# Latent attention with its queries and keys made token by token, latent norms as token factors, and the in-projection's tiles in another order

## The chip, the cores and the metric

One core of a Trainium2 chip runs the whole program; nothing is shared with other cores. The metric is the device time of one execution in microseconds, a median over runs. The engines are named as in the profile: PE (matrix products; PEld is its weight load), DVE and ACT (elementwise work), POOL (here it only splits weights), SP (a queue that issues DMA).

## The reference

A residual stream x of 512 tokens and 1024 channels passes through two layers of a first block (attention with an indexer, two recurrences, SwiGLU networks) and two layers of a second. The change lies in the first layer of the second block, in its latent attention (`mla_qkv` and the short convolution beside it):

```python
p_lat, p_ctx = h_lat @ w_in, h_ctx @ w_in          # 512 and 256 tokens; 384 + 256 + 32 latent columns, 3 x 512 for the convolution
q  = (rmsnorm(cq,  q_norm_g)  @ w_uq ).reshape(B, T, 8, 96)
kv = (rmsnorm(ckv, kv_norm_g) @ w_ukv).reshape(B, T, 8, 64 + 64)
k  = concat([k_nope, broadcast(k_pe)])             # 64 columns per head, 32 that all heads share
q, k = rmsnorm(q, q_gain), rmsnorm(k, k_gain)      # over the 96 columns of a head
# latent tokens only: axial rope on the last 32 columns of q and k
# attention of 512 queries over 512 + 256 keys
# short_conv: z = c_gate * u; y = 3 taps of z along tokens; b_gate * y
```

All is float32. A norm of a latent is a factor per token and a gain per column, so the factor can be applied before the following product or after it.

## The kernel before, in words

Activations lie with channels on the partitions: a buffer h has 8 chunks of 128 channels by 512 tokens. Every product is made of three (`products`, lines 1810 to 1815): operands are split in a rounded high part and the remainder, and high x high, high x low, low x high are added in PSUM. Weights come as one stream of tiles of 128 x 1024 (512 KB). SP loads tile t into slot t % 4 of `w_raw` once `w_used` says that the tile four places back was consumed (line 445); ACT rounds it to `w_hi` (`round_tile`, L480), at a place in ACT's program written out by hand; POOL subtracts and gives `w_lo` (L458). PE takes a tile with 24 products of 512 columns (`linear_tile`).

Latent attention is the functions `mla` of ACT (from line 897), DVE (1660) and PE (2411). The order on each engine is written out by hand, and the engines meet in semaphores.

**In-projection**, 18 tiles, in order 0 to 17. After the norm of x, `first_tiles` makes tiles 0 and 1. PE then adds the squares of the 8 context chunks with a product with ones (L2419). From that sum ACT takes a root (L912), DVE a reciprocal (L1668) and scales and shifts the context (L1670, L1673), ACT rounds it (L914), DVE subtracts (L1676). Tiles 2, and then 3 to 5, which also have 24 products of 256 columns for the context (`linear_ctx`), follow; ACT evicts each bank (L918, L921). Tiles 0 to 2 are the query latent, 3 and 4 the key and value latent, 5 the shared rope columns. ACT squares both latents (L925, L926), PE adds the squares per token (L2445), ACT and DVE make root and reciprocal (L940, L941, L1682), PE spreads the factors over the partitions (L2458), DVE scales the latents (L1687), ACT rounds (L945, L947), DVE subtracts (L1691). Tiles 6 to 17 are the convolution, three to a group of 128 channels; ACT evicts the first (L935), DVE multiplies it with the second (L1700), makes the taps (L1702, L1704) and multiplies with the third (L1706). Since DVE's work on the latents stands ahead of the first convolution in its program, and PE reuses the banks, tile 10 waits for L1700.

**Queries and keys.** For each of 8 query heads (512 tokens, 9 products) and 8 key heads (768 tokens, 12 products) the weight is the stationary side, so a head comes out with its 96 columns on the partitions. Then per head: ACT evicts (L964, L967) and squares (L975), PE adds the squares per token (L2470), ACT takes the root (L982), DVE the reciprocal (L1724), PE spreads the factor over 96 partitions (L2480), DVE scales (L1728), PE makes the rotated columns (L2490), DVE applies rope with three operations (L1717 to L1719). PE's steps of head i - 1, i - 2 and i - 3 stand behind the products of head i. The key half alone waits on the copy L1709. Then the values: six blocks of 128 tokens as the stationary side, 6 products each (L2532 to L2534), evicted by ACT (L995).

**Attention**, 32 pairs of a token block and a head: scores (L2546, L2547), maximum (L1750, L1751), exponential (L1005), six turns (L2553), product with the values (L2561).

Of the kernel before, what the change touches and what calls it, by code (L numbers as in the profile page):

```python
# [19 lines left out]
P = 128  # L20
T = 512
D = 1024
KD = D // P
# [83 lines left out]
def build_program(nc, io, out):  # L107
# [3 lines left out]
    with ExitStack() as ctx:  # L111
# [238 lines left out]
        ctx_x = flat2[:, 0:KD * CTX].rearrange("p (k t) -> p k t", k=KD)  # L350
        cq = mem2[:, 4:7, :]
        ckv = flat2[:, 7 * T:7 * T + 2 * TK].rearrange("p (c t) -> p c t", c=2)
# [8 lines left out]
        consts2 = core_mem[:, 12:15, :].rearrange("p u t -> p (u t)")[:, 0:N_CONSTS_2]  # L361
# [7 lines left out]
        def qk_width(i):  # L369

            return T if i < 8 else TK


        def qk_tok(i):

            return head_tok[:, KB * (i % 2):KB * (i % 2) + qk_width(i) // P]
# [14 lines left out]
        def ada_cols(layer, part, which=0):  # L391
# [24 lines left out]
            "lat_sq", "lat_sum", "lat_std", "lat_f", "lat_hi", "lat_ready", "c_out", "u_taken", "conv_taken",  # L416
            "qk_ready", "qk_out", "qk_sq", "qk_sum", "qk_std", "qk_inv", "qk_spread", "qk_done", "lat_inv", "lat_spread", "kpe_ready", "rot2_ready", "rot2_done", "vtok_ready", "vtok_out",
# [5 lines left out]
        def _(sp):  # L423
# [18 lines left out]
            with sp.Fori(1, stream_tiles // RING) as i:  # L442
# [19 lines left out]
        def _(act):  # L462
# [434 lines left out]
            def mla(order, updates):  # L897
                base = BASE["mla_in"]

                def load_ctx():  # L900

                    act.wait_ge(S["x_ready"], KD * updates)
                    act.dma_start(ctx_x, io["ctx_t"].rearrange("(k p) t -> p k t", p=P)).then_inc(S["ctx_loaded"], 16)

# [3 lines left out]
                for m in range(6):  # L908
                    if m == 2:

                        act.wait_ge(S["ctx_sum"], 1)
                        nc.scalar.activation(mem2[:, CTX_STD, 0:CTX], ps[:, 6, 0:CTX], ACT.Sqrt, scale=1.0 / D, bias=eps(EPS_NORM)).then_inc(S["ctx_std"], 1)  # L912
                        act.wait_ge(S["ctx_f"], 1)
                        nc.scalar.activation(hc_hi[:, :, :], ctx_x, ACT.Copy).then_inc(S["ctx_hi"], 1)  # L914
                    act.wait_ge(S["w_used"], base + m + 1)
                    bank = ps[:, m % 2, :]
                    out = cq[:, m, :] if m < 3 else ckv[:, m - 3, 0:T] if m < 5 else kpe[:, 0:T]
                    nc.scalar.activation(out, bank, ACT.Copy).then_inc(S["proj_out"], 1)  # L918
                    if m >= 3:
# [1871 lines left out]
```

## Time and profile before

| | us |
|---|---|
| median of 3 runs | 3841.18 (3839.13 to 3841.76) |
| the profiled execution, its own time | 3836.46 |
| its span, first to last instruction | 3834.7 |
| PE busy | 3595.0 (94%) |
| DVE, ACT, POOL busy | 1614.7, 1240.5, 1237.4 |
| latent attention's in-projection, from tile 2 on | 134.2 |
| its queries, keys and values | 124.2 |
| its attention | 114.1 |
| mean granted clock of PE | 0.952 of full |

The profiled execution is 4.7 us below the median of the runs. Times in rows count from the start of the span. PE's durations overlap, since products are pipelined; the distance of two starts is what one costs. "idle before" is the time an engine stood before an instruction, with what ended it. A granted clock of 1.00 is 2.4 GHz, 0.50 is 1.2 GHz.

### The profile page before, as it was taken

Reading aid. Unit: us, or ns where it says so; the run is one execution under the profiler, and the core shown is the slowest. Engines: PE = TensorE matmul, PEld = TensorE weight load, DVE = VectorE, ACT = ScalarE, POOL = GpSimd, SP = SyncE. Lnnn points to the kernel's source line nnn. Section 1 sums busy time; section 2 is a strip of 40 time slices with the busy share of each in tenths; the row PEclk is TensorE's granted clock in tenths of the full one; section 3 lists DMA queues with packets and bytes.
Section 4 is the critical chain, followed back from the end, with each engine's and each line's share of the span. In section 5 each row is a group of like instructions: output and inputs, shape, how many; then the busy total and the mean of one; then the engine's idle time right before and its main releaser. Section 6 shows DMA issues by size and latency. Waiting matters only on the chain.

```text
span 3834.7 us, 46792 instructions
## 1 busy us (share of the span) xinstructions
PE 3595.0 (94%) x17424; PEld 2954.8 (77%) x17424; DVE 1614.7 (42%) x2716; ACT 1240.5 (32%) x1852; POOL 1237.4 (32%) x516
## 2 busy tenths in 40 slices
PE   7999997689999999999778999988899999989999
PEld 6888775588888888877557888867677888777887
DVE  5440596656331433168575533123555221323220
ACT  3222435234222322243522422232233332323331
POOL 3444330004444444433000444423102444323443
PEclk9999996799999999999779999989899999999999
DMA  4442220003442344222000344222001222112222
GB/s 169 148 144 97 77 83 6 1 1 122 143 145 104 138 143 147 93 77 77 6 1 1 127 148 143 104 72 75 26 6 45 103 94 99 66 61 88 94 98 93
DMA packets 93534, 332.08 MB, mean 87 GB/s; under 512 B 10432, under 2 KB 12128, under 8 KB 93280
## 3 DMA queue, kind: packets, MB, share of 16 engines
q1 hardware_dynamic: 77136, 274.65, 20.5%
q10 hardware_dynamic: 16272, 55.65, 4.2%
q8 instruction: 91, 1.49, 0.2%
q14 instruction: 35, 0.29, 0.0%
HBM read 327.64 MB, written 2.62 MB: 86 GB/s over the span
## 4 chain that ended last, share of the span: by engine, by line
PE 86%; DVE 9%; ACT 2%; issue 2%; DMA 1%; SPq 0%; DVEq 0%; ACTq 0%
PE ps L1813 22%; PE ps L1815 21%; PE ps L1814 21%; PE ps L1834 1%; PE ps L1839 1%; PE ps L1835 1%; DMA w_raw<-in_tiles 1%; PE ps L2561 1%; PE ps L1964 1%; PE ps L2116 1%; PE ps L2546 1%; DVE mem L1254 1%; DVE stat L1253 1%; PE ps L1957 1%; PE ps L2295 1%
## 5 line engine op out<-in xcount | busy, mean ns | idle before, releaser
L458 POOL TENSOR_TENSOR w_lo<-w_raw,w_hi 128x1024 fp32r<-128x1024 f32 x512 | 1237.2, 2418 | 2573.8 <-ACT w_hi L480 2573.5
L1813 PE MATMUL ps<-h_hi,w_hi 128*128 128x512 f32 x2656 | 1044.7, 393 | 8.9 <-DVE mem L1700 7.0
L1815 PE MATMUL ps<-h_hi,w_lo 128*128 128x512 f32 x2656 | 1034.9, 390 | 0.0
L1814 PE MATMUL ps<-h_lo,w_hi 128*128 128x512 f32 x2656 | 1034.5, 389 | 0.0
L480 ACT ACTIVATE w_hi<-w_raw 128x1024 fp32r<-128x1024 f32 x512 | 540.8, 1058 | 990.5 <-DMA w_raw<-in_tiles 985.6
L1813 PEld LDWEIGHTS ps<-h_hi,w_hi 128*128 128x128 f32 x2656 | 499.4, 188 | 127.7 <-issue 14.3
L1814 PEld LDWEIGHTS ps<-h_lo,w_hi 128*128 128x128 f32 x2656 | 499.6, 188 | 105.3 <-issue 3.4
L1815 PEld LDWEIGHTS ps<-h_hi,w_lo 128*128 128x128 f32 x2656 | 499.2, 188 | 104.8
L1159 DVE TENSOR_TENSOR a_lo<-sil,a_hi 128x512 f32 (+1 forms) x132 | 298.6, 2262 | 492.7 <-ACT a_hi L622 492.7
L1813 PE MATMUL ps<-a_hi,w_hi 128*128 (+1 forms) x1056 | 410.8, 389 | 0.0
L1814 PE MATMUL ps<-a_lo,w_hi 128*128 (+1 forms) x1056 | 410.8, 389 | 0.0
L1815 PE MATMUL ps<-a_hi,w_lo 128*128 (+1 forms) x1056 | 410.8, 389 | 0.0
L614 ACT ACTIVATE sil<-ps 128x512 f32<-128x512 f32 x129 | 77.1, 598 | 698.9 <-PE ps L1815 690.2
L1157 DVE TENSOR_TENSOR sil<-sil,ps 128x512 f32<-128x512 f32 x129 | 88.7, 688 | 392.9 <-ACT sil L614 392.9
L1814 PEld LDWEIGHTS ps<-a_lo,w_hi 128*128 128x128 f32 x1056 | 198.2, 188 | 41.5
L1813 PEld LDWEIGHTS ps<-a_hi,w_hi 128*128 128x128 f32 x1056 | 198.2, 188 | 40.9
L1815 PEld LDWEIGHTS ps<-a_hi,w_lo 128*128 128x128 f32 x1056 | 198.2, 188 | 40.9
L1188 DVE SCALAR_TENSOR_TENSOR x<-ps,x 128x512 f32<-128x512 f32 x32 | 22.1, 692 | 310.4 <-PE ps L1815 309.8
L1136 DVE SCALAR_TENSOR_TENSOR ada_raw<-ada_raw,sq 128x1024 f32<-128x1024 f32 x96 | 126.2, 1317 | 9.5 <-DMA ada_raw<-in_ada_tiles 9.5
L1834 PE MATMUL ps<-h_hi,w_hi 128*128 128x512 f32 x208 | 87.9, 423 | 17.3 <-DVE h_lo L1082 8.8
L1188 DVE SCALAR_TENSOR_TENSOR x<-ps,ada,x 128x512 f32<-128x512 f32 x16 | 12.0, 751 | 193.0 <-PE ps L1815 193.0
L1835 PE MATMUL ps<-h_hi,w_lo 128*128 128x512 f32 x208 | 85.9, 413 | 0.0
(448 smaller groups left out, 3913.0 us busy)
## 6 DMA issues: line engine op xcount, KB each, us to landing
w_raw<-in_tiles SPq DMA_DIRECT2D x512, 512.0 KB, 3.2
ada_raw<-in_ada_tiles ACTq DMA_DIRECT2D x96, 512.0 KB, 3.2
x<-in_x_t SPq DMA_DIRECT2D x2, 1024.0 KB, 6.5
sq<-in_cond ACTq DMA_DIRECT2D x4, 512.0 KB, 4.2
out_t<-x SPq DMA_DIRECT2D x1, 2048.0 KB, 7.1
consts<-in_consts SPq DMA_DIRECT2D x1, 1280.0 KB, 12.8
mem<-in_ctx_t ACTq DMA_DIRECT2D x1, 1024.0 KB, 8.7
core_mem<-in_consts ACTq DMA_DIRECT2D x1, 576.0 KB, 3.8
```

Of the source, the lines that this page charges most:

```text
L458: nc.gpsimd.tensor_tensor(w_lo[:, s, :], w_raw[:, s, :], w_hi[:, s, :].bitcast(F32), ALU.subtract).then_inc(S["w_lo_ready"], 1)
L480: nc.scalar.activation(w_hi[:, t % RING, :], w_raw[:, t % RING, :], ACT.Copy).then_inc(S["w_hi_ready"], 1)
L614: nc.scalar.activation(sil[:, j, :], ps[:, 2 * j, :], ACT.Silu).then_inc(S["silu_ready"], 1)
L1136: nc.vector.scalar_tensor_tensor(raw, raw, 1.0, cond_rows(n)[0], ALU.mult, ALU.mult, accum_out=ada[:, 0, column]).then_inc(S["ada_used"], 1)
L1157: nc.vector.tensor_tensor(sil[:, j, :], sil[:, j, :], ps[:, 2 * j + 1, :], ALU.mult).then_inc(S["af_ready"], 1)
L1159: nc.vector.tensor_tensor(a_lo[:, 2 * i + j, :], sil[:, j, :], a_hi[:, 2 * i + j, :].bitcast(F32), ALU.subtract).then_inc(S["a_ready"], 1)
L1253: link(nc.vector.max(top, score(n)))
L1813: nc.tensor.matmul(bank, wh, hi, start=first, stop=False, skip_group_check=True)
L1814: nc.tensor.matmul(bank, wh, lo, start=False, stop=False, skip_group_check=True)
L1815: return nc.tensor.matmul(bank, wl, hi, start=False, stop=last, skip_group_check=True)
L1834: nc.tensor.matmul(ps[:, banks[r], :], w_hi[:, slot, block], h_hi[:, k, :], start=(n == 0), stop=False, skip_group_check=True)
L1835: nc.tensor.matmul(ps[:, banks[r], :], w_lo[:, slot, block], h_hi[:, k, :], start=False, stop=False, skip_group_check=True)
```

## The change

Order and buffers of the in-projection: the tiles come in the order 0, 1, 2, 6, 7, 8, 3, 4, 5, 9 to 17 (the SP queue writes out the loads of that stretch, all others stay in loops). Each latent goes to a bank of its own; ACT writes its high part straight from the bank with the norm's gain as the scale, and its squares beside it; DVE makes the low part from the bank (`low_part`). The token factor isn't applied to the latents. DVE adds the context's squares over chunks, so that PE needs one product, and likewise the latents' squares. The tables for rope and their gains are turned to tokens on the partitions by 14 small turns and 2 products of PE into bank 7, and DVE multiplies them with the gains once; the table load is issued on ACT's queue right behind the context's.

Queries and keys: 20 units. A query unit is 128 tokens by 4 heads (384 columns, 9 products, 8 units), a key unit 128 tokens by 8 heads (512 columns, 6 products, 6 units), a value unit as before. Latents are the stationary side, weights the moving one, read in pieces of 96 or 64 columns across two slots. Per unit: ACT squares the bank, DVE sums over a head's columns, ACT takes the root (with the latent's factor as scale, for keys with the shared columns' sum as bias), DVE inverts it and scales the bank into tokens, and applies rope on 32 columns of each head (queries), or multiplies the ready roped key columns by the factor (keys). PE turns each head back to columns on the partitions, two units late, and ACT evicts the turn with the head's gain. The value eviction carries the latent's factor. Weight tiles are rounded by ACT at the units in `rounds`; two or more slots are freed at once by the units in `UNITS_LAST`.

```diff
-        ctx_x = flat2[:, 0:KD * CTX].rearrange("p (k t) -> p k t", k=KD)
...
+        ctx_x = flat2[:, 16 * T:16 * T + KD * CTX].rearrange("p (k t) -> p k t", k=KD)
...
-        consts2 = core_mem[:, 12:15, :].rearrange("p u t -> p (u t)")[:, 0:N_CONSTS_2]
+        consts2 = flat2[:, 4 * T:4 * T + N_CONSTS_2]
...
+        MLA_ORDER = (0, 1, 2, 6, 7, 8, 3, 4, 5, *range(9, 18))
+        LATENT_BANKS = ((0, None), (1, None), (3, None), (4, 6), (5, 7), (4, 6))
+        Q_UNITS, K_UNITS, V_UNITS = 8, KB, KB
+        QK_UNITS = Q_UNITS + K_UNITS
...
+            return (3, 0, 1, 2)[u % 4]
+        UNITS_LAST = {3: 2, 7: 4, 13: 6, 19: 7}
...
+            for t in range(RING * first_group, RING * (last_group + 1)):
+                source = base + MLA_ORDER[t - base] if t in reordered else t
+                sp.wait_ge(S["w_used"], t + 1 - RING)
+                sp.dma_start(w_raw[:, t % RING, :], io["tiles"][source]).then_inc(w_loaded[t % RING], 16)
...
+                def latent(m):
+                    bank, ctx_bank = LATENT_BANKS[m]
+                    if m < 3:
+                        nc.scalar.activation(cq_hi[:, m, :], ps[:, bank, :], ACT.Copy, scale=param("mla_qn", m))
+                        nc.scalar.activation(mem2[:, CQ_STD + m, :], ps[:, bank, :], ACT.Square).then_inc(S["lat_taken"], 1)
+                    elif m < 5:
+                        for part, source in ((slice(0, T), ps[:, bank, :]), (slice(T, TK), ps[:, ctx_bank, 0:CTX])):
+                            nc.scalar.activation(ckv_hi[:, m - 3, part], source, ACT.Copy, scale=param("mla_kvn", m - 3))
+                            ins = nc.scalar.activation(ckv_sq[:, m - 3, part], source, ACT.Square)
+                        ins.then_inc(S["lat_taken"], 1)
...
+                for p, m in enumerate(MLA_ORDER):
+                    act.wait_ge(S["w_used"], base + p + 1)
+                    if m < 6:
+                        latent(m)
+                    elif m % 3 == 0:
+                        j = (m - 6) // 3
+                        if j >= 2:
+                            act.wait_ge(S["u_taken"], j - 1)
+                        nc.scalar.activation(mem2[:, j % 2, :], ps[:, 0, :], ACT.Copy).then_inc(S["c_out"], 1)
+                    if p == 2:
                         act.wait_ge(S["ctx_sum"], 1)
                         nc.scalar.activation(mem2[:, CTX_STD, 0:CTX], ps[:, 6, 0:CTX], ACT.Sqrt, scale=1.0 / D, bias=eps(EPS_NORM)).then_inc(S["ctx_std"], 1)
+                    if p == 3:
                         act.wait_ge(S["ctx_f"], 1)
                         nc.scalar.activation(hc_hi[:, :, :], ctx_x, ACT.Copy).then_inc(S["ctx_hi"], 1)
...
+                    if p < 16:
+                        round_tile(base + p + 4)
...
+                rounds = {0: (2,), 2: (3,), 6: (4,), 7: (5,), 9: (6,), 10: (7,)}
...
+                    if u >= 2:
+                        act.wait_ge(S["qk_sum"], u - 1)
+                    nc.scalar.activation(unit_squares(u), unit_products(u), ACT.Square).then_inc(S["qk_sq"], 1)
+                    act.wait_ge(S["qk_sum"], u + 1)
+                    n = u % TB if u < Q_UNITS else TB + u - Q_UNITS
+                    bias = eps(EPS_NORM) if u < Q_UNITS else kpe_bias[:, n - TB:n - TB + 1]
+                    nc.scalar.activation(unit_sums(u), unit_sums(u), ACT.Sqrt, scale=lat_factor2[:, n:n + 1], bias=bias).then_inc(S["qk_std"], 1)
+                def turned_out(u):
+                    for x, turn in enumerate(turns(u)):
+                        act.wait_ge(S["qk_turned"], turn + 1)
+                        if u < Q_UNITS:
+                            out = mem2[0:QKD, Q_MLA + 4 * (u // TB):Q_MLA + 4 * (u // TB) + 4, blk(u % TB)]
+                        else:
+                            out = kmla[0:QKD, 4 * x:4 * x + 4, blk(u - Q_UNITS)]
+                        gain = gains[0:QKD, int(u >= Q_UNITS):int(u >= Q_UNITS) + 1]
+                        nc.scalar.activation(out, heads(ps[0:QKD, 4 + turn % 4, :]), ACT.Copy, scale=gain).then_inc(S["qk_out"], 1)
...
+                    if 2 <= u < QK_UNITS + 2:
+                        turned_out(u - 2)
+                    for t in rounds.get(u, ()):
+                        round_tile(base + t)
+                for t in (8, 9, 10):
+                    round_tile(base + t)
...
+                    if m < 3:
+                        ins = V.scalar_tensor_tensor(cq_lo[:, m, :], ps[:, bank, :], param("mla_qn", m), cq_hi[:, m, :].bitcast(F32), ALU.mult, ALU.subtract)
+                    else:
...
+                low_part(0)
+                low_part(1)
+                dve.wait_ge(S["ctx_sq"], 1)
+                link(V.tensor_tensor(ctx_sq[:, 0:4, :], ctx_sq[:, 0:4, :], ctx_sq[:, 4:8, :], ALU.add))
+                link(V.tensor_tensor(ctx_sq[:, 0:2, :], ctx_sq[:, 0:2, :], ctx_sq[:, 2:4, :], ALU.add))
+                V.tensor_tensor(ctx_sq[:, 0, :], ctx_sq[:, 0, :], ctx_sq[:, 1, :], ALU.add).then_inc(S["ctx_added"], 1)
+                low_part(2)
...
+                def rope_tokens(x, cos, sin, temp, n):
+                    link(V.tensor_tensor(temp, x, sin, ALU.mult))
+                    link(V.tensor_tensor(x, x, cos, ALU.mult))
+                    V.tensor_tensor(halves(x, 0), halves(x, 0), halves(temp, 1), ALU.subtract)
+                    return V.tensor_tensor(halves(x, 1), halves(x, 1), halves(temp, 0), ALU.add)
...
+                conv(0)
+                low_part(3)
+                low_part(4)
+                square = lambda c: mem2[:, CQ_STD + c, :]
+                link(V.tensor_tensor(square(0), square(0), square(1), ALU.add))
+                V.tensor_tensor(square(0), square(0), square(2), ALU.add)
+                V.tensor_tensor(ckv_sq[:, 0, :], ckv_sq[:, 0, :], ckv_sq[:, 1, :], ALU.add).then_inc(S["lat_added"], 1)
...
+                for u in range(QK_UNITS):
+                    h, inv, tok, source = unit_heads(u), unit_sums(u), unit_tokens(u), unit_products(u)
+                    n = u % TB if u < Q_UNITS else TB + u - Q_UNITS
+                    factor = lat_factor[:, n:n + 1]
+                    dve.wait_ge(S["qk_sq"], u + 1)
+                    V.reduce_sum(inv, unit_squares(u), AX_X).then_inc(S["qk_sum"], 1)
+                    dve.wait_ge(S["qk_std"], u + 1)
+                    link(V.reciprocal(inv, inv))
+                    if u >= 2:
+                        dve.wait_ge(S["qk_turned"], turns(u - 2)[-1] + 1)
+                    spread = lambda w: inv.unsqueeze(2).to_broadcast([P, h, w])
+                    if u < Q_UNITS:
+                        V.scalar_tensor_tensor(tok, source, factor, spread(QKD), ALU.mult, ALU.mult).then_inc(S["qk_scaled"], 1)
+                        dve.wait_ge(S["qk_scaled"], u + 1)
+                        rope_tokens(tok[:, :, HD:QKD], over(cos_gain[:, n, :], h), over(sin_gain[:, n, :], h), by_head(rope_temp, 4), h).then_inc(S["qk_done"], 1)
+                    else:
+                        V.scalar_tensor_tensor(tok[:, :, 0:HD], source, factor, spread(HD), ALU.mult, ALU.mult).then_inc(S["qk_scaled"], 1)
+                        V.tensor_tensor(tok[:, :, HD:QKD], over(kpe_roped[:, n - TB, :], h), spread(32), ALU.mult).then_inc(S["qk_done"], 1)
...
+                    if p == 3:
+                        pe.wait_ge(S["ctx_added"], 1)
+                        nc.tensor.matmul(ps[:, 6, 0:CTX], const("ones"), ctx_sq[:, 0, :], start=True, stop=True).then_inc(S["ctx_sum"], 1)
+                    if m < 6:
+                        bank, ctx_bank = LATENT_BANKS[m]
+                        if m >= 3:
+                            pe.wait_ge(S["ctx_ready"], 1)
+                            pe.wait_ge(S["w_lo_ready"], t + 1)
+                            if m == 5:
+                                pe.wait_ge(S["lat_lo"], 4)
+                            linear_ctx(ps[:, ctx_bank, 0:CTX], t)
+                        linear_tile(ps[:, bank, :], t)
+                    else:
+                        j, part = (m - 6) // 3, (m - 6) % 3
+                        if j == 0 and part < 2:
+                            pe.wait_ge(S["lat_lo"], part + 1)
+                        if j:
+                            pe.wait_ge(S[("c_out", "u_taken", "conv_taken")[part]], j)
+                        linear_tile(ps[:, part, :], t)
...
+                    if u >= 4:
+                        if u - 4 < QK_UNITS:
+                            pe.wait_ge(S["qk_scaled"], u - 3)
+                        else:
+                            pe.wait_ge(S["vtok_out"], u - 4 - QK_UNITS + 1)
...
+                        half, n = divmod(u, TB)
+                        pe.wait_ge(S["w_lo_ready"], base + 2 * half + 2)
+                        out = bank[:, 0:4 * QKD].rearrange("p (s h d) -> p s h d", s=2, h=2)
+                        weights = lambda w, k: w[:, 2 * half:2 * half + 2, 0:6 * P].rearrange("p s (h k m) -> p s h k m", h=2, k=3)[:, :, :, k, 0:QKD]
+                        chunks, hi, lo = 3, cq_hi, cq_lo
...
+                    for k in range(chunks):
+                        nc.tensor.matmul(out, hi[:, k, blk(n)], weights(w_hi, k), start=(k == 0), stop=False)
+                        nc.tensor.matmul(out, hi[:, k, blk(n)], weights(w_lo, k), start=False, stop=False)
+                        ins = nc.tensor.matmul(out, lo[:, k, blk(n)], weights(w_hi, k), start=False, stop=(k == chunks - 1))
+                    if u in UNITS_LAST:
...
+                def turn(u):
+                    pe.wait_ge(S["qk_done"], u + 1)
+                    for x, slot in enumerate(turns(u)):
+                        if slot >= 4:
+                            pe.wait_ge(S["qk_out"], slot - 3)
+                        for h in range(4):
+                            ins = nc.tensor.transpose(ps[0:QKD, 4 + slot % 4, blk(h)], unit_tokens(u)[:, 4 * x + h, :], const("ident"))
+                        ins.then_inc(S["qk_turned"], 1)
...
+                for u in range(QK_UNITS + V_UNITS):
+                    if u == 1:
+                        pe.wait_ge(S["c_out"], 4)
+                    if u == 2:
+                        pe.wait_ge(S["u_taken"], 4)
+                    if u == 3:
+                        pe.wait_ge(S["conv_taken"], 4)
+                    products_of(u)
+                    if 2 <= u < QK_UNITS + 2:
+                        turn(u - 2)
...
```

## Rows read from the trace of the kernel before

**Rows 1.** The page: the chain that ended last, share of the span by engine

```profile
PE 86%; DVE 9%; ACT 2%; issue 2%; DMA 1%; SPq 0%; DVEq 0%; ACTq 0%
```

**Rows 2.** Stretches: length, busy us (count) per engine, granted clock, DMA share, GB/s

```profile
2531.50:2665.70 134.20, 114.08 (x542) 96.20 (x540) 34.93 (x49) 32.26 (x38) 40.68 (x17) 0.91 0.19 67
...
2665.70:2789.90 124.20, 108.70 (x556) 81.73 (x556) 55.20 (x81) 35.61 (x61) 17.96 (x8) 0.89 0.11 35
...
2789.90:2904.00 114.10, 109.47 (x720) 89.47 (x720) 67.36 (x104) 35.62 (x70) 2.34 (x1) 0.99 0.02 6
...
740.00:760.00 20.00, 13.77 (x122) 13.15 (x121) 16.00 (x56) 4.04 (x9) 0.00 (x0) 0.83 0.00 1
...
1890.00:1970.00 80.00, 49.88 (x213) 35.91 (x211) 44.24 (x125) 32.32 (x51) 0.00 (x0) 0.59 0.02 7
```

**Rows 3.** Timeline, PE, in-projection: start us, us, instruction, [idle before <-releaser]

```profile
2531.45 3.62 PE L2419 MATMUL ps<-mem,consts 128*128 128x256 f32 x16
...
2551.12 0.55 PE L1813 MATMUL ps<-hc_hi,w_hi 128*128 128x256 f32 x1 [10.60 <-issue]
...
2578.79 0.47 PE L1813 MATMUL ps<-h_hi,w_hi 128*128 128x512 f32 x1 [1.01 <-ACT mem L918]
...
2585.10 7.37 PE L2445 MATMUL ps<-consts,mem 128*128 128x1 f32 x48 [0.60 <-ACT mem L926]
...
2604.69 2.39 PE L2458 MATMUL ps<-consts,head_tok 128*128 128x128 f32 x20
...
2619.57 0.80 PE L1813 MATMUL ps<-h_hi,w_hi 128*128 128x512 f32 x1 [7.02 <-DVE mem L1700]
...
2659.64 0.39 PE L1815 MATMUL ps<-h_hi,w_lo 128*128 128x512 f32 x1
...
2664.40 0.39 PE L1815 MATMUL ps<-h_hi,w_lo 128*128 128x512 f32 x1
```

**Rows 4.** Timeline, ACT and DVE, in-projection, around the context's normalisation

```profile
2535.60 1.06 ACT L480 ACTIVATE w_hi<-w_raw 128x1024 fp32r<-128x1024 f32 x1 [3.58 <-DMA w_raw<-in_tiles]
...
2538.49 1.75 DVE L1668 RECIPROCAL mem<-mem 128x256 f32<-128x256 f32 x1 [9.66 <-ACT mem L912]
...
2548.73 2.29 DVE L1676 TENSOR_TENSOR hc_lo<-mem,hc_hi 128x2048 fp32r<-128x2048 f32 x1 [1.98 <-ACT hc_hi L914]
```

**Rows 5.** Waits of DVE, 2665.7 to 2790: us in total, times, longest

```profile
DVE mem L1717 <- PE ps L2490: 49.1, 16, 4.4
```

**Rows 6.** Groups by line, DVE, whole span: count, busy us, mean ns, idle before

```profile
L1750 DVE TENSOR_REDUCE stat<-ps 128x1 f32<-128x768 f32 x32 | 30.6, 958 | 48.0 <-PE ps L2547 47.9
...
L1728 DVE SCALAR_TENSOR_TENSOR mem<-mem,params,ps 96x512 f32<-96x512 f32 x8 | 5.9, 744 | 3.2 <-PE ps L2480 3.0
...
L1724 DVE RECIPROCAL head_tok<-head_tok 128x4 f32<-128x4 f32 x8 | 1.4, 169 | 6.8 <-ACT head_tok L982 6.8
...
L1478 DVE SCALAR_TENSOR_TENSOR mem<-ps,stat,consts 128x128 f32<-128x128 f32 x32 | 8.4, 343 | 0.0
...
L1719 DVE TENSOR_TENSOR mem<-mem 32x512 f32<-32x512 f32 x8 | 5.5, 683 | 0.3
```

**Rows 7.** Groups by line, ACT, 2505 to 2904: the root of a head's sums

```profile
L982 ACT ACTIVATE head_tok<-ps,consts 128x4 f32<-128x4 f32 x8 | 2.0, 251 | 0.2 <-PE ps L2470 0.2
```

**Rows 8.** Timeline, PE: turns of 128x128 and products of 512 at both clocks

```profile
2795.80 0.88 PE L2553 MATMUL ps<-consts,mem 128*128 128x128 f32 x6 [3.04 <-ACT mem L1005]
...
2798.91 1.39 PE L2553 MATMUL ps<-consts,mem 128*128 128x128 f32 x6
...
2701.91 0.63 PE L1815 MATMUL ps<-cq_hi,w_lo 128*128 128x512 f32 x1
...
2702.34 0.63 PE L1813 MATMUL ps<-cq_hi,w_hi 128*128 128x512 f32 x1
```

**Rows 9.** Timeline, POOL and DVE: a split and a rope operation that met

```profile
2731.19 2.68 POOL L458 TENSOR_TENSOR w_lo<-w_raw,w_hi 128x1024 fp32r<-128x1024 f32 x1 [19.32 <-ACT w_hi L480]
...
2731.67 2.74 DVE L1719 TENSOR_TENSOR core_mem<-core_mem,mem 32x512 f32<-32x512 f32 x1
```

More of the change, by code:

```diff
@@ L907, in mla @@
                 nc.scalar.activation(ctx_sq, ctx_x, ACT.Square).then_inc(S["ctx_sq"], 1)
[L908 to L919, printed above, removed]
-                        out = ckv[:, m - 3, T:TK] if m < 5 else kpe[:, T:TK]
-                        nc.scalar.activation(out, ps[:, 2 + m % 2, 0:CTX], ACT.Copy).then_inc(S["ctx_out"], 1)
-                    round_tile(base + m + 4)
@@ L977, in qk_std @@
-                def qk_std(i):
-                    act.wait_ge(S["qk_sum"], i + 1)
-                    if i >= 2:
-                        act.wait_ge(S["qk_spread"], i - 1)
-                    nc.scalar.activation(qk_tok(i), ps[:, 6, 0:qk_width(i) // P], ACT.Sqrt, scale=1.0 / QKD, bias=eps(EPS_NORM)).then_inc(S["qk_std"], 1)
-                for i in range(16):
-                    qk(i)
-                    if i:
-                        qk_std(i - 1)
-                qk_std(15)
-                t = BASE["mla_kv"] + 2
@@ L990, in mla @@
-                for n in range(6):
-                    if n < 5:
-                        act.wait_ge(S["vtok_ready"], n + 1)
-                    else:
-                        act.wait_ge(S["w_used"], t + 1)
-                    nc.scalar.activation(vtok[:, n, :], ps[:, n % 4, :], ACT.Copy).then_inc(S["vtok_out"], 1)
-                round_tile(t + 4)
+                    if p == 2:
+                        act.wait_ge(S["ctx_sum"], 1)
+                        nc.scalar.activation(mem2[:, CTX_STD, 0:CTX], ps[:, 6, 0:CTX], ACT.Sqrt, scale=1.0 / D, bias=eps(EPS_NORM)).then_inc(S["ctx_std"], 1)
@@ L1721, in mla @@
-                for i in range(16):
-                    head = mem2[0:QKD, Q_MLA + i, :] if i < 8 else kmla[0:QKD, i - 8, :]
-                    dve.wait_ge(S["qk_std"], i + 1)
-                    V.reciprocal(qk_tok(i), qk_tok(i)).then_inc(S["qk_inv"], 1)
-                    if i:
-                        rotate(i - 1)
-                    dve.wait_ge(S["qk_spread"], i + 1)
-                    V.scalar_tensor_tensor(head, head, param("q_gain" if i < 8 else "k_gain")[0:QKD, :], psf[0:QKD, 4 * T:4 * T + qk_width(i)],
-                                           ALU.mult, ALU.mult).then_inc(S["qk_done"], 1)
@@ L2537, in mla @@
+                for u in range(QK_UNITS + V_UNITS):
+                    if u == 1:
[7 more added lines that the diff above has]
+                        turn(u - 2)
+                pe.wait_ge(S["qk_out"], Q_UNITS + 2 * K_UNITS)
                 pe.wait_ge(S["vtok_out"], 6)
```

324 lines of the change are left out of this document (140 added, 184 removed).

## The prediction

> **What bounds the kernel now.** I read the chain of waits on the page first: PE is 86% of what ended last [rows 1], so a change pays where PE waits or does work that it need not do. Next the stretches [rows 2]: the in-projection of the latent attention from 2531.5 us (134.2 us), its queries, keys and values from there to the first scores at 2789.9 us (124.2 us), and the attention itself (114.1 us at a granted clock of 0.99). The first two run at 0.91 and 0.89, and together they are 258 us of 3834.7: all that the change touches. Then PE's timeline [rows 3] for what it does there beside streaming weights, and the waits [rows 5]. The price rows are [rows 6] to [rows 9].
>
> In the in-projection PE adds the context's squares with 16 records (3.62 us), stands 10.60 us until the context rows are normalised, adds the latents' squares with 48 small records (7.37 us, after a wait of 0.60), spreads the latent factors with 20 (2.39 us), and stands 7.02 us for DVE's first convolution product, which is queued behind the latents' split [rows 3]. In the query and key part each of 16 heads has a chain PE, ACT, PE, ACT, DVE, PE, DVE, PE (product, square, sum, root, reciprocal, spread, scale, rotate): DVE waits 49.1 us in 16 waits for the rotation product [rows 5], yet PE, issuing all these small pieces, is what the stretch is made of (108.7 busy us of 124.2) [rows 2].
>
> **In-projection, part by part** (the 16 tiles of 24 products that follow the first two, and the three context products, are the same work as before and leave the sum). Removed: context squares added on DVE first, so 2 records are left of 16, 3.62 - 0.45 = 3.2; the stop of 10.6, because three convolution tiles now stand ahead of the first tile that needs the context; 28 of 48 small records, 7.37 x 28/48 = 4.3, with the 0.6 ahead of them; the spread, 2.4; the stop of 7.0, as the first latents' low parts come straight from PSUM. A wait of 1.01 us for an evicted bank goes with them, since each latent now has its own bank. Sum 29.1.
>
> Added: (a) a new stop at the context sum. ACT takes latent 0, then rounds the next weight tile, which lands late: that rounding ends at 2536.66 [rows 4]. Latent 1 (a copy and a square, about 1.2) is queued behind it, then DVE's low part of it (0.75) and three additions of 1024, 512 and 256 elements (about 2.3 by [rows 6]): 2540.9. PE is through tile 2 at 2531.45 + 24 x 0.227 = 2536.9 (0.227 from 21 steps between 2659.64 and 2664.40) [rows 3]. Stop 4.0. Behind PE's wait stands everything, behind ACT's rounding only the latent. (b) 14 turns of rope tables and 2 gain spreads, 18 records at no more than 7.37/48 = 0.154: 2.8; below, 0.12 each by the spread's 2.39/20 [rows 3]. (c) DVE's table work, about 4 us ahead of the second convolution, covered by the tile PE is at; were the cover gone it is 4 us. (d) 576 KB of tables on ACT's queue behind the context's load, and the SP queue written out for the reordered tiles: 512 KB each as before, nothing. The context's normalisation lasts 12.5 us as before (2538.49 to 2551.02) [rows 4]; started at 2541.9 it ends at 2554.4, while PE, after the sum and three tiles of 5.4, asks at 2557.7. Cover 3.3 us. Two of three slow restarts (about eight products at 0.427 instead of 0.227 [rows 8]) go: 3.2. Net 29.1 - 4.0 - 2.8 + 3.2 = **25.5 us**.
>
> **Queries, keys, values.** Now latents are the stationary side: 8 query units (128 tokens, 4 heads, 9 products of 384 columns), 6 key units (8 heads, 6 products of 512), 6 value units. PE per query unit: 9 x 0.170 (0.227 x 384/512) plus 4 turns at 0.147 [rows 8] = 2.1; per key unit 6 x 0.227 + 8 x 0.147 = 2.5. The sums are DVE reductions, the spreads and rotation products are gone.
>
> DVE per query unit: reduction of 384 0.56 (0.96 for 768 less 384 x 1.04 ns; that slope from 0.343 at 128 and 0.744 at 512), root on ACT 0.25 with 0.16 of handing over, reciprocal 0.17, scaling 384 0.61, rope two operations of 128 at 0.34 and two of 64 at 0.28, less overlap: 3.0 [rows 6, 7]. Key unit: 0.69 + 0.41 + 0.17 + 0.74 + 0.48 and gaps, 2.55. So DVE sets the pace, ACT (square, root, one or two copies, a rounding) fits under it. Sum:
> lead of unit 0, products and square, 2.2;
> 8 x 3.0 = 24.0;
> a wait for the key weights. The second key tile is rounded at the end of unit 7's turn on ACT: after the root a copy 0.6, the rounding 1.06, POOL 2.7, products 1.4, square 0.6 = 6.3 against DVE's 2.1: 4.2 [rows 4, 9];
> 6 x 2.55 = 15.3;
> POOL. A rope operation with both inputs in SBUF took 0.68, but 2.74 where it met a split that ended with it (2731.19 + 2.68, 2731.67 + 2.74) [rows 9]. Six splits fall here, which bounds this between nothing and 6 x 2.68 = 16; I take 4, since rope is a third of DVE's time and two splits fall into waits;
> clock 5, between 0 and 14 (below);
> last turns 1.2, four value units 5.4, a copy 0.6: 7.2.
> Together 61.9; 124.2 - 61.9 = **62.3 us**. The roundings ahead of the first exponential existed before.
>
> What is not shown: a moving operand in four runs of 96 and stride-0 second inputs. Both bounds: no dearer than the rows, or the ordinary rate (a rival).
>
> Total 87.8 us. Profiled execution 3836.46, so 3748.7; the median lies 4.7 above that execution: **3753 us**. A measurement here tells 0.2% (about 8 us) from no change.
>
> **Where page and trace differ.** PE would be busy 2.1 of 3.0 us per query unit. The nearest rows: 13.77 busy of 20 us at a clock of 0.83, but also 49.88 of 80 at 0.59 [rows 2]; the second has long gaps, mine are under 1 us, so I stand nearer the first. The Trainium skill, TensorE: Matmul & The Clock Gate, section A second HAM failure mode, says that frequent short idling between groups of matmuls, cycling through PSUM banks, makes the clock swing between its two levels; that speaks against this change and is the first rival.
>
> **Rivals.** (1) PE falls to 1.2 GHz in the new part and becomes the bound: query unit 9 x 0.32 + 4 x 0.23 = 3.8, key unit 6 x 0.427 + 8 x 0.23 = 4.4 [rows 8], values 4 x 2.6. That is 8 x 0.8 + 6 x 1.85 + 5 = 22, less the 5 taken: 3770. For it the 0.59 row, against it that denser work lifts the clock back. Chance 0.15. (2) DVE is dearer: port waits up to their bound of 16 (+12) and 0.4 us more per unit in linked small operations (+5): 3770. Chance 0.17. (3) The operand in four runs goes at the rate of the old spreads, two records or 0.24 us per 128 columns [rows 3]: 9 x 0.72 + 0.6 = 7.1 per query unit, 6 x 0.96 + 1.2 = 7.0 per key unit, PE sets the pace, 8 x 4.1 + 6 x 4.4 = +59: 3812. Nothing in the trace is near it; 0.03. (4) Slower: the sparse new part leaves the clock low, and attention and its out-projection (114.1 us at 0.99 now, then some 44) run at 1.2 GHz: 158 x 0.88 = +139, 3892. It decides once more than 108 us of dense work stay slow; against it, the slow stretch at 2701.91 ended after nine products. 0.01. (5) The change doesn't shorten the chain, because a wait is merely renamed (the key weights arrive a full tile later each time): within 0.2%, 0.02. (6) No clock or port cost, no wait for the context sum: -13, 3740. 0.12.
>
> **How the numbers follow.** The forecast case has 0.50. Its range with (1), (2) and (6) is 3730 (case 6 with 10 us of cheaper rope) to 3785 (both dear cases, partly added). Left out: (3), (4), (5) and some overrun, under 0.2. Faster 0.96, same 0.02, slower 0.02.
>
> **What would show it.** Right: the in-projection near 109 us with one stop of about 4 us ahead of the context sum, none of 10.6 or 7.0; 14 DVE turns 2.5 to 3 us apart; one wait of about 4 us between units 7 and 8; first scores some 62 us after the last in-projection tile. Wrong: query units over 3.5 us apart, a clock under 0.75 there, or a stop of over 2 us inside the convolution tiles.

## The result, and the profile of the changed kernel

| | before | after |
|---|---|---|
| median, us | 3840.6 (3839.13 to 3841.76, 4 runs) | 3755.69 (3750.93 to 3764.14, 4 runs) |
| the profiled execution | 3836.46 | 3750.93 |
| in-projection, behind tile 1 to the last tile | 134.23 | 109.91 |
| queries, keys, values, to the first score | 124.25 | 63.22 |
| everything else in the span | 3576.2 | 3576.0 |

The ratio is 0.9782 (95%: 0.9763 to 0.9800): faster. The last three lines come from one profiled execution each, cut at PE's first record behind tile 1 (before, the first of the context's squares; after, the first product of tile 2), at the first query product and at the first attention score. The two stretches gave 24.3 and 61.0 us, 85.3 together, and the rest of the program did not move. The same cuts serve for all runs below. They tell more than the median: in two of the experiments the profiled execution was 15 to 20 us longer in parts that no edit touches.

Windows of the changed kernel: length, busy us (count) of PE, PEld, DVE, ACT, POOL, granted clock, DMA share, GB/s. They answer to [rows 2].

```profile
2528.90:2639.00 110.10, 104.58 (x499) 87.58 (x498) 43.30 (x69) 29.47 (x40) 40.80 (x16) 0.95 0.24 82
2639.00:2702.04 63.04, 44.77 (x225) 37.63 (x224) 38.80 (x81) 33.02 (x61) 14.27 (x6) 0.86 0.16 59
...
2702.00:2816.00 114.00, 109.40 (x720) 89.49 (x720) 67.27 (x104) 37.19 (x71) 6.96 (x3) 0.99 0.02 6
```

In the second line PE is busy 45 of 63 us where it was busy 109 of 124; no engine is near full, so a chain sets the time. Summed from start to start and without the stops, PE's small records (squares' sums, spreads, rotations, turns) fell from 60.4 to 9.5 us, and the products from 48.3 to 35.5: the new units stream fewer columns, and PE's busy time fell by some 12.9 us in the products themselves. Attention keeps its clock of 0.99.

PE's timeline of the changed kernel, the records before which it stood 0.8 us or more in both stretches (the figure in brackets is the time it stood):

```profile
2540.03 1.22 PE L2529 MATMUL ps<-mem,consts 128*128 128x256 f32 x2 [5.53 <-DVE mem L1751]
...
2646.31 0.65 PE L2610 MATMUL ps<-consts,mem 128*96 128x128 f32 x4 [2.48 <-DVE mem L1789]
...
2654.06 0.54 PE L2595 MATMUL ps<-w_hi,cq_hi 128*128 128x384 f32 x1 [3.80 <-POOL w_lo L531]
...
2673.36 0.76 PE L2595 MATMUL ps<-w_hi,ckv_hi 128*128 128x512 f32 x1 [9.25 <-POOL w_lo L531]
...
2689.07 1.08 PE L2610 MATMUL ps<-consts,mem 128*96 128x128 f32 x8 [1.25 <-DVE mem L1840]
...
2702.04 1.10 PE L2634 MATMUL ps<-core_mem,mem 96*128 96x512 f32 x2 [0.87 <-ACT mem L1059]
```

The stops of 10.60 and 7.02 [rows 3] are gone, and one of 5.53 stands ahead of the context's sum. In the second stretch PE waits for DVE, and twice (3.80, 9.25) for weights that were rounded and split late. To see the pace, read DVE's timeline: two query units of the changed kernel, the second of which met a weight split.

```profile
2660.53 0.55 DVE L1828 TENSOR_REDUCE stat<-sq 128x4 f32<-128x384 f32 x1
2661.53 0.18 DVE L1830 RECIPROCAL stat<-stat 128x4 f32<-128x4 f32 x1 [0.46 <-ACT stat L1035]
2661.74 0.62 DVE L1835 SCALAR_TENSOR_TENSOR mem<-ps,head_tok,stat 128x384 f32<-128x384 f32 x1
2662.40 0.29 DVE L1786 TENSOR_TENSOR mem<-mem 128x128 f32<-128x128 f32 x1
...
2663.33 0.55 DVE L1828 TENSOR_REDUCE stat<-sil 128x4 f32<-128x384 f32 x1
...
2665.85 0.23 DVE L1788 TENSOR_TENSOR mem<-mem 128x64 f32<-128x64 f32 x1
2665.99 2.36 DVE L1789 TENSOR_TENSOR mem<-mem 128x64 f32<-128x64 f32 x1
2668.28 0.54 DVE L1828 TENSOR_REDUCE stat<-sq 128x4 f32<-128x384 f32 x1
```

A free unit takes 2663.33 - 2660.53 = 2.80 us, without a wait but for the 0.46 of the root on ACT. The next takes 4.95, since its last rope operation lasted 2.36 instead of 0.22: POOL's split ran from 2665.89 to 2668.27. The eight reductions start at 2641.33, 2646.17, 2648.97, 2653.92, 2657.72, 2660.53, 2663.33 and 2668.28, so three such meetings are paid on the path (2.04, 2.15 and 2.15). One wait of 0.93 for the second pair of query tiles lies at 2657.72. A fourth meeting (2670.93) lies inside the wait for the key weights:

```profile
2657.72 0.55 DVE L1828 TENSOR_REDUCE stat<-sil 128x4 f32<-128x384 f32 x1 [0.93 <-ACT sil L1031]
...
2670.93 2.36 DVE L1789 TENSOR_TENSOR mem<-mem 128x64 f32<-128x64 f32 x1
...
2676.92 0.69 DVE L1828 TENSOR_REDUCE stat<-sil 128x8 f32<-128x512 f32 x1 [3.63 <-ACT sil L1031]
```

The first key unit starts 8.64 after the last query unit, 5.84 more than a free unit.

### The profile page after: what moved, and what is told of

It is laid out like the page before. It is cut to its first block, busy times and chain, and to the rows that moved or that the text cites. A ratio compares the mean times of both kernels' runs of the same rounds, so it can differ in the third digit from the quotient of the medians.

```text
span 3749.1 us, 45994 instructions
## 1 busy us (share of the span) xinstructions
PE 3520.1 (94%) x17048; PEld 2901.3 (77%) x17048; DVE 1607.8 (43%) x2737; ACT 1236.8 (33%) x1855; POOL 1236.7 (33%) x516
## 4 chain that ended last, share of the span: by engine, by line
issue 54%; PE 27%; POOL 17%; DVE 1%; ACT 1%; POOLq 0%; DMA 0%; SPq 0%; DVEq 0%
POOL w_lo L531 17%; PE ps L1921 7%; PE ps L1923 7%; PE ps L1922 7%; PE ps L2649 1%; PE ps L2634 1%; PE ps L2641 1%; PE ps L1942 1%; PE ps L1943 0%; PE ps L1947 0%; PE ps L2695 0%; PE ps L2697 0%; PE ps L2696 0%; PE ps L2635 0%; POOLq L530 0%
## 5 line engine op out<-in xcount | busy, mean ns | idle before, releaser
L1942 PE MATMUL ps<-h_hi,w_hi 128*128 128x512 f32 x208 | 88.7, 427 | 17.3 <-ACT h_hi L643 12.3
```

What stands on the lines that cost most here:

```text
L1942: nc.tensor.matmul(ps[:, banks[r], :], w_hi[:, slot, block], h_hi[:, k, :], start=(n == 0), stop=False, skip_group_check=True)
```

## Experiments

Each edit is on the changed kernel, but for one on the kernel before. B is the in-projection and C the query, key and value stretch of the profiled execution. Runs of the kernel before beside them had medians of 3838.99 (9 runs, for the first four) and 3839.17 (11 runs, for the others); ratios are against these.

### The order of the tiles alone undone (`order_old`)

```diff
-        MLA_ORDER = (0, 1, 2, 6, 7, 8, 3, 4, 5, *range(9, 18))
+        MLA_ORDER = tuple(range(18))
...
-                    if p == 3:
+                    if p == 2:
                         act.wait_ge(S["ctx_f"], 1)
```

(DVE's `conv(0)` goes behind its low parts and sums of the latents.)

> The changed kernel with its tiles in the old order 0 to 17. ACT rounds the context directly behind its root, and DVE makes the first convolution product behind the latents, as the old order needs. Theory (the order hides the context's normalisation): the changed kernel has 13.5 us between the context sum at 2541.2 us and the end of the context's low part at 2554.7, and this order lets PE stand all of it, with about 1.5 us of slow products behind. In-projection about 125 us instead of 109.9, total about 15 us over the changed kernel's 3755.7, so 3771. Rival (the order only moves the stop, the rest of the gain comes from the direct low parts and the shorter sums): within 4 us of 3755.7.

3766.99 (3764.78 to 3778.73), ratio 0.9819 (0.9799 to 0.9839). B is 121.24, 11.3 more than with the new order, and C 63.72. PE's timeline of this kernel:

```profile
2544.77 1.22 PE L2529 MATMUL ps<-mem,consts 128*128 128x256 f32 x2 [5.64 <-DVE mem L1751]
...
2558.13 0.58 PE L1921 MATMUL ps<-hc_hi,w_hi 128*128 128x256 f32 x1 [12.14 <-DVE hc_lo L1764]
```

The stop for the normalised context is back, at 12.14. So the new order hides that normalisation and no other wait; the stop ahead of the context's sum is there with either order. The 11.3 are less than the 15 expected. The stop is 1.4 shorter than reckoned. Some 2.3 us of slow products stand behind it (23 products of 256 columns at 0.213 in place of 0.120), but the 3.8 us of slow products that the next experiment finds in the changed kernel do not occur here.

### The context's additions ahead of the latents' low parts (`adds_first`)

```diff
-                low_part(0)
-                low_part(1)
                 dve.wait_ge(S["ctx_sq"], 1)
                 ...
                 V.tensor_tensor(ctx_sq[:, 0, :], ctx_sq[:, 0, :], ctx_sq[:, 1, :], ALU.add).then_inc(S["ctx_added"], 1)
+                low_part(0)
+                low_part(1)
```

> DVE adds the context's squares before it makes the low parts of latents 0 and 1, nothing else moved. Theory: the 5.53 us stop of PE ahead of the context sum is DVE's order alone (low part 1 waits for ACT, which has a late rounding ahead of it; the second addition then meets POOL's split and takes 2.71 us instead of 0.7). The squares are ready at about 2527.5, so the sum is ready before PE is through tile 2: stop gone or under 0.5, and up to 1.5 us of slow products with it. In-projection 103 to 105 us instead of 109.9, total 5 to 7 us less: 3749 to 3751. Rival: the low parts now come late, and PE stops by the same amount ahead of tile 6 or 7, which need banks 0 and 1: total unchanged, a stop of about 5 us one tile later.

3742.07 (3739.67 to 3746.05), ratio 0.9749 (0.9733 to 0.9765). B is 100.19, 9.7 less, and C 63.06. The stop is gone, as the theory says, but the gain is nearly twice the stop. Rows of DVE's and POOL's timeline in the changed kernel:

```profile
2533.31 5.66 POOL L531 TENSOR_TENSOR w_lo<-w_raw,w_hi 128x1024 fp32r<-128x1024 f32 x2 [17.14 <-ACT w_hi L553]
...
2534.33 0.75 DVE L1740 SCALAR_TENSOR_TENSOR cq_lo<-ps,params,cq_hi 128x512 fp32r<-128x512 f32 x1 [3.49 <-ACT mem L988]
2535.00 1.77 DVE L1749 TENSOR_TENSOR mem<-mem 128x1024 f32<-128x1024 f32 x1
...
2536.80 2.71 DVE L1750 TENSOR_TENSOR mem<-mem 128x512 f32<-128x512 f32 x1
2539.55 0.42 DVE L1751 TENSOR_TENSOR mem<-mem 128x256 f32<-128x256 f32 x1
```

And the same additions in this kernel:

```profile
2527.17 1.23 DVE L1747 TENSOR_TENSOR mem<-mem 128x1024 f32<-128x1024 f32 x1 [1.05 <-ACT mem L981]
2528.43 0.69 DVE L1748 TENSOR_TENSOR mem<-mem 128x512 f32<-128x512 f32 x1
...
2529.16 0.42 DVE L1749 TENSOR_TENSOR mem<-mem 128x256 f32<-128x256 f32 x1
```

The additions were ready to run at 2527 and stood behind DVE's wait for ACT (3.49) until 2535, when POOL was splitting: 4.9 us of work in place of 2.3. The rest of the gain is clock. Behind the stop the changed kernel's first product took 0.79 and eight more were 0.43 apart instead of 0.227, and some 51 us on, about 1 us behind the last of the 20 one-column products of the latents' sums, nine products were slow again (0.31 to 0.43); adds_first has the 20 products too but neither slow stretch. Windows over the latter place, from about 1 us behind those 20 products, where both kernels stream the same weights, changed kernel first and adds_first second:

```profile
2592.75:2596.00 3.25, 3.25 (x9) 2.48 (x8) 0.00 (x0) 0.96 (x1) 0.00 (x0) 0.50 0.04 11
```

```profile
2584.40:2587.65 3.25, 3.25 (x16) 2.67 (x15) 0.00 (x0) 1.06 (x1) 0.72 (x1) 1.00 0.03 10
```

From start to start, the stop with the sum's own product takes 6.2 us in the changed kernel where that product alone takes 0.25 here, and the two slow stretches lie 2.2 and 1.6 above the distance of 0.227. That accounts for the 9.7.

### The second key tile's and its neighbour's roundings earlier (`rounds_early`)

```diff
-                rounds = {0: (2,), 2: (3,), 6: (4,), 7: (5,), 9: (6,), 10: (7,)}
+                rounds = {0: (2,), 2: (3,), 4: (4,), 5: (5,), 9: (6,), 10: (7,)}
```

> ACT rounds the two key weight tiles after units 4 and 5 instead of 6 and 7. Theory: PE's 9.25 us stop ahead of the first key unit and DVE's 3.63 us are the place of that rounding; the tiles have landed by then. DVE's wait goes, and with it 3.6 us plus about 1.5 us of products at the low clock: queries, keys and values 58 to 60 us instead of 63.2, total 3 to 5 less: 3751 to 3753. Rival: the splits then fall on rope operations of units 5 and 6 (each had cost 2.1 us where it met one), which gives back what the wait gave: within 1.5 us of 3755.7.

3746.71 (3745.55 to 3762.53), ratio 0.9759 (0.9743 to 0.9774). B 109.85, C 59.13: 4.1 less. The wait of DVE between the last query unit and the first key unit is gone (the two reductions are 2.80 apart instead of 8.64); the gain is smaller than 5.84 because the split that lay in that wait is now met on the path, as the rival expected, so that four query units instead of three take 4.8 to 5.0. The two stretches hold 4.1 us of gain, while the median is 9.0 below the changed kernel's; the rest lies where the edit touches nothing and is not claimed. DVE's timeline of this kernel:

```profile
2687.49 0.55 DVE L1828 TENSOR_REDUCE stat<-sq 128x4 f32<-128x384 f32 x1
...
2690.29 0.68 DVE L1828 TENSOR_REDUCE stat<-sil 128x8 f32<-128x512 f32 x1
```

The wait came from where the rounding stood in ACT's program, not from the load of the weights.

### Rope tables and scratch in PSUM (`psum_tables`)

```diff
-        cos_gain, sin_gain = (by_head(flat2[:, at:at + TB * 32], TB) for at in (10 * T + TK, 10 * T + TK + TB * 32))
-        rope_temp = flat2[:, T + 256:T + 384]
+        cos_gain, sin_gain = (by_head(ps[:, 7, at:at + TB * 32], TB) for at in (0, TB * 32))
+        rope_temp = ps[:, 7, 256:384]
```

(The turns then cycle through three banks, 4 to 6, in place of four.)

> The gained rope tables and the scratch of rope go to PSUM bank 7, turns use three banks instead of four; rope operations of query units then have one input in SBUF and one in PSUM. Theory (a DVE operation with both inputs in SBUF waits for a split by POOL): four rope operations of 0.2 to 0.3 us took 2.32, 2.36, 2.36 and 2.36 in the changed kernel; all are 0.3 us here, query part 6.2 us shorter, of which the last 2 us were hidden by the wait for the key weights: total 4 us less, 3751 to 3752. Rival (they wait for something else, such as the semaphore): still four operations over 2 us, no change. Three banks for turns cost nothing, because two turns are at most under way. The Trainium skill, SBUF - State Buffer, section Who interferes with whom, says that an operation of VectorE with two SBUF inputs contends with a GpSimd instruction that reads SBUF, and one with at most one such input outside the two-port modes does not; that is the theory's side.

3751.36 (3747.53 to 3753.88), ratio 0.9769 (0.9753 to 0.9786). B 109.81, C 60.78: 2.4 less. POOL's and DVE's timeline of this kernel, at the split that cost unit 0 its 2.04 before:

```profile
2646.94 2.38 POOL L531 TENSOR_TENSOR w_lo<-w_raw,w_hi 128x1024 fp32r<-128x1024 f32 x1 [8.24 <-ACT w_hi L553]
```

```profile
2646.81 0.30 DVE L1786 TENSOR_TENSOR ps<-mem,ps 128x128 f32<-128x128 f32 x1
2647.15 0.29 DVE L1787 TENSOR_TENSOR mem<-mem,ps 128x128 f32<-128x128 f32 x1
2647.47 0.22 DVE L1788 TENSOR_TENSOR mem<-mem,ps 128x64 f32<-128x64 f32 x1
2647.61 0.21 DVE L1789 TENSOR_TENSOR mem<-mem,ps 128x64 f32<-128x64 f32 x1
...
2659.36 0.55 DVE L1828 TENSOR_REDUCE stat<-sil 128x4 f32<-128x384 f32 x1 [3.06 <-ACT sil L1031]
```

Four operations ran at their ordinary 0.2 to 0.3 us beside the split, the first begun 0.13 us ahead of it: with one input in PSUM they do not meet POOL at all. This is what the Trainium skill, SBUF — State Buffer, section Who interferes with whom, states (a DVE operation with two SBUF inputs contends with a POOL instruction that reads SBUF, one with a single SBUF input does not), and the trace agrees: the second rope operation (L1787) took 2.32 us with both inputs in SBUF, the first row below from the changed kernel, and 0.29 with one. But of the 6.3 us of meetings only 2.4 came back. DVE, now early, waits 3.06 for the second pair of query tiles (0.93 in the changed kernel) and longer for the keys (5.75 against 3.63); by its last reduction it is 3.5 us ahead. Then 1.0 is lost again: from the last reduction to the first score this kernel takes 10.98 (all_three below, with three banks too, 10.99) and the changed one 9.94. So three banks for the turns, which were expected to cost nothing, have a price: PE now stands in the middle of a key unit's turns until ACT has evicted one, the second row, from this kernel. That the total came out as expected (3751 to 3752) is therefore luck.

```profile
2643.54 2.32 DVE L1787 TENSOR_TENSOR mem<-mem 128x128 f32<-128x128 f32 x1
```

```profile
2688.40 0.64 PE L2610 MATMUL ps<-consts,mem 128*96 128x128 f32 x4 [1.26 <-ACT core_mem L1046]
```

### DVE's reductions twice, PE's turns twice (`dve_double`, `pe_double`)

```diff
+                    if u < Q_UNITS:
+                        link(V.reduce_sum(inv, unit_squares(u), AX_X))
                     V.reduce_sum(inv, unit_squares(u), AX_X).then_inc(S["qk_sum"], 1)
```

```diff
-                        for h in range(4):
+                        for h in (*range(4), *range(4)) if u < Q_UNITS else range(4):
```

> The changed kernel, each query unit's reduction made twice in a row by DVE (8 more of 0.55 us, linked, 0.6 each). Theory (DVE sets the pace of the units): 8 x 0.6 = 4.8 us longer, less up to 1.5 where a wait for weights covers it (units 3 and 7): 3.3 to 4.8, so 3759 to 3760.5. Rival (PE or ACT sets the pace): under 1 us.

> The changed kernel, each query unit's four turns made twice (PE gets 8 x 0.5 us more, DVE nothing). Theory (DVE sets the pace, PE has about 0.9 us to spare per unit): under 1 us longer, within 1 us of 3755.7. Rival 1 of the prediction (PE is the bound): 4 us and more. A third outcome, PE's fuller units keep its clock higher and the part becomes shorter, would show as a granted clock over 0.9 where it was 0.86.

dve_double: 3756.85 (3755.26 to 3767.19), ratio 0.9786 (0.9769 to 0.9804), C 67.14. pe_double: 3754.32 (3752.18 to 3767.80), ratio 0.9781 (0.9761 to 0.9800), C 63.68. Windows over C, dve_double first:

```profile
2640.54:2707.68 67.14, 46.01 (x226) 38.71 (x224) 43.17 (x89) 33.05 (x61) 14.27 (x6) 0.85 0.15 55
```

```profile
2639.94:2703.61 63.67, 48.50 (x257) 42.08 (x256) 38.77 (x81) 33.21 (x61) 14.29 (x6) 0.87 0.16 58
```

4.4 us more for DVE made C 3.9 longer; 3.7 us more for PE made it 0.45 longer. In the query units DVE sets the pace and PE does not. ACT's work was not doubled, and in the key units DVE waits 0.3 to 1.3 us for ACT's squares, so for these the pace isn't DVE's alone. The medians show neither apart from the changed kernel's own scatter: these two rest on the stretch of one execution each.

### The old kernel's spreads twice (`spread_twice`, on the kernel before)

```diff
-                    for n in range(qk_width(i) // P):
+                    for n in (*range(qk_width(i) // P), *range(qk_width(i) // P)):
```

> The kernel before, each head's factor spread twice by PE (8 times 4 and 8 times 6 more products of 128 columns, 160 records, at 0.12 to 0.15 us each: 20 to 24 us of PE). Theory (the old query and key part was made of PE's small pieces): 18 to 24 us longer than before's 3840.6, so about 3861. Rival (it was made of the round trips to ACT and DVE, PE stood in between): under 8 us, since PE's pieces of the next head would cover it.

3866.88 (3863.50 to 3872.95), ratio 1.0069 (1.0054 to 1.0085). B 134.14, C 151.57: 27.3 more, over the 18 to 24 expected. PE's busy time grew by 22.9 (108.7 to 131.57) for 160 more records. So the small pieces lay on the path, and the rival (under 8 us) is out: their removal is the main part of what the change gained there. The other 4.4 us are PE's stops, 20.0 in place of 15.6, where it waits longer for a head's factor (L2480 for DVE's L1724, 12.4 us in place of 5.6).

### The three remedies together (`all_three`)

adds_first and psum_tables, with the roundings at units 0, 1, 4, 5, 9 and 10.

> The additions first, the tables in PSUM, and the roundings of weight tiles 3, 4 and 5 after units 1, 4 and 5. Theory: the three parts add up: 6 (additions) + 4 to 6 (port) + 3 to 5 (key weights, and 0.9 for the second query pair) = 13 to 17 us less than 3755.7: 3739 to 3743, queries, keys and values 52 to 54 us. Rival (they hide one another, the parts of a chain that DVE's pace sets): 8 us or less, 3748.

3735.41 (3731.87 to 3749.33), ratio 0.9722 (0.9706 to 0.9739). B 100.18, C 50.96, a little better than the 3739 to 3743 and 52 to 54 expected. It beats both kernels; its slowest run (3749.33) is below the changed kernel's fastest (3750.93), and the medians stand as 3735.41 / 3755.69 = 0.995. Window over C:

```profile
2647.93:2698.89 50.96, 42.29 (x226) 34.90 (x224) 30.23 (x81) 32.79 (x61) 14.16 (x6) 0.97 0.20 73
```

C fell by 12.3, where rounds_early and psum_tables alone gave 4.1 and 2.4: alone, each let DVE run into the next meeting or wait. The parts are not quite the same: tile 3 is rounded behind unit 1 here and behind unit 2 in rounds_early, so how much of the difference is that was not tested by itself. DVE's reductions are 2.8 to 2.9 us apart here in all eight query units, and the 1.0 of the three banks is still paid.

## Why the prediction was right, and where its terms were off

3753 was forecast and 3755.69 measured, inside 3730 to 3785, by the forecast case. The mechanism held: the stops and small pieces went, and DVE sets the pace of the query units. Several sizes were off and mostly cancelled, so that a miss of under 3 us is in part luck. Of its own signs, two did not come out as written. Only 6 of the 13 distances between DVE's reductions lie in 2.5 to 3 us, and the eight query units are 3.85 us apart on average, which the sign "over 3.5 us apart" calls wrong. The units as such took 2.80; the rest are the splits and the wait, of which the sum had priced the splits as a term of their own.

**In-projection, 25.5 forecast, 24.3 measured.** The removed stops went as argued, and the context's normalisation stayed covered. These terms were mis-sized. (a) The stop ahead of the context's sum was 5.53, not 4.0. The chain named was the right one (rounding, latent 1, its low part, additions) and started about 1 us earlier than reckoned, but the additions took 4.9 instead of 2.3, as two of them ran beside POOL's splits. The prediction priced that contention for rope and forgot it here. (b) "Two of three slow restarts go" was wrong: two stretches of slow products are left, one of them where PE does not stop at all. Products above their full pace cost 5.8 us before and 4.5 after, so 1.3 came back and not 3.2. (c) The 18 small records of the rope tables took 1.4 us from start to start, not 2.8 (two rows, 1.06 and 0.61, that overlap), and (d) the 20 of the latents' sums 2.15 (a row of 2.29, ends included), against 3.1 at the 0.154 taken from [rows 3]. (e) The context's 16 squares had cost 3.3 from start to start, not their row's 3.62, and the sum's product, slow behind the stop, costs 0.7: 2.6 came back and not 3.2; the spread's 20 had cost 2.15, not 2.4. (f) A wait of 0.9 ahead of the old kernel's first query product is gone and was not in the sum. Together: 25.5 - 1.5 - 1.9 + 1.4 + 0.8 - 0.6 - 0.3 + 0.9 = 24.3. The rows for (c) and (d), PE's timeline of the changed kernel:

```profile
2589.73 2.29 PE L2550 MATMUL ps<-consts,mem 128*128 128x1 f32 x20
...
2599.14 1.06 PE L2561 MATMUL ps<-consts,mem 32*128 32x32 f32 x14
2600.05 0.61 PE L2563 MATMUL ps<-consts,params 32*128 32x32 f32 x4
```

The larger error is one that the total does not show: the stop was given 4 us where removing it gives 9.7. The cheapest remedy of the case, two lines moved, was therefore undervalued.

**Queries, keys and values, 61.9 forecast, 63.2 measured.** By the starts of DVE's reductions:

| term | forecast | measured |
|---|---|---|
| lead of unit 0 | 2.2 | 2.5 |
| 8 query units | 8 x 3.0 = 24.0 | 8 x 2.80 = 22.4 |
| splits met | 4 | 6.3 (three), a fourth inside the key wait |
| wait for the second pair of query tiles | none | 1.0 |
| key weights, over a free unit | 4.2 | 5.8 |
| 6 key units | 15.3 | 17.65 |
| tail | 7.2 | 7.5 |
| clock | 5 | in the terms above |

The clock's 5, which the measured terms hold already, stood in for what the other terms missed, 6.3 together; that is why the sum is only 1.3 off. The forecast counted a unit's busy times well. Left out were ACT's roundings between key units (3.15 and 3.72 us for two of them, 2.77 for the others) and the query tiles' own late weights. The clock cost less than 5: some 1.5 of it lies in the key wait, where six products after the stop of 9.25 were 0.43 to 0.56 apart. The rows, PE's timeline of the changed kernel:

```profile
2673.92 0.63 PE L2596 MATMUL ps<-w_lo,ckv_hi 128*128 128x512 f32 x1
2674.35 0.63 PE L2597 MATMUL ps<-w_hi,ckv_lo 128*128 128x512 f32 x1
```

**The rivals.** (1) PE bound at the low clock: the clock did fall to 0.86 on average, but PE was busy only 45 of 63 us and adding to it cost little (pe_double). The rule of the Trainium skill, TensorE: Matmul & The Clock Gate, section A second HAM failure mode, is borne out in that the granted clock went from 1.00 to 0.50 three times in this part with its many short waits; it did not decide the time. With the waits shortened the clock was 0.97 (all_three). (2) DVE dearer: port waits 2.3 over the term taken, far from its bound of 16, and units cheaper; no. (3) The operand in four runs costs nothing that matters: products of 384 columns start 0.18 us apart, against 0.170 by proportion.

```profile
2660.49 0.34 PE L2596 MATMUL ps<-w_lo,cq_hi 128*128 128x384 f32 x1
2660.67 0.34 PE L2597 MATMUL ps<-w_hi,cq_lo 128*128 128x384 f32 x1
```

(4) Attention ran at 0.99, as before. (5) A wait was not merely renamed: C halved. (6) No stop and no port cost: this is what all_three comes near, 3735 against the 3740 given, though it also lacks the wait for the key weights, which this case kept.

## What to carry to other kernels

Where PE is busy with many one-column or spread pieces per head, keep tokens on the partitions so that a norm is a reduction and a factor per partition. After such a change look again at the order on each engine: work that is ready but queued behind a wait is cheap to move (the three additions, stop 5.5, gave 9.7 us; the two roundings, wait 5.8, gave 4.1). Put one input of a DVE operation in PSUM where POOL runs beside it, but clear the next wait at the same time, or little comes back.

## What the runs showed of the hardware that was not expected

- **A stop cost more than its length here.** 5.5 us of standing cost 9.7: slow products right behind it, and a second slow stretch some 51 us later, while PE stands nowhere (clock 0.50 there, 1.00 in the kernel without the stop). B was 109.8 to 109.9 in all five profiled executions with the new tile order and the stop, and 100.2 in both without it, so this is no scatter. The second stretch begins in all five about 1 us behind the last of the 20 one-column products. In the two kernels without the stop these are followed by none, and neither are they in order_old, which has two stops (5.64 and 12.14): a stop alone does not bring it. Why the clock falls the second time is open. In the kernel before it is at 0.50 in the middle of 48 one-column products, with PE busy throughout:

```profile
2589.00:2592.00 3.00, 3.00 (x16) 3.00 (x15) 0.00 (x0) 0.00 (x0) 2.25 (x1) 0.50 0.00 0
```

- **The root with two operands per token.** With a scale and a bias from memory it took 0.39 us on ACT, where the old one [rows 7] took 0.251. The Trainium skill, ScalarE: Activation LUTs, section What ACT_TABLE_LOAD costs, gives some 93 ns for each such operand; here one more, the scale, came with 0.14 more. No run here separates the operand from the change of source from PSUM to SBUF. Over 14 units in the chain it makes some 2 us.
